# A chunkwise matrix memory: all increments of the state at once in three banks, seven states kept, one denominator step for eight chunks

## The chip, the cores and the metric

The kernel runs on one core of one Trainium2 chip. The metric is the device time of one execution in microseconds (us); lower is better. TensorE (PE) multiplies matrices and transposes, VectorE (DVE) and ScalarE (ACT) work elementwise, GpSimd (POOL) does a little, SyncE (SP) issues the transfers.

## The reference, cut to what matters

Two transformer blocks follow each other on 1024 tokens of width 1024, in float32. The first block has windowed attention beside a matrix memory (mLSTM), then cross attention and a gated feed-forward layer; the second has an RWKV-7 mixer beside banded attention. The change touches the matrix memory alone, which has 4 heads of width 128:

```python
    def step(carry, inp):
        C, n, m = carry
        ...
        num = (w_inter[..., None] * jnp.einsum('bhtd,bhde->bhte', qc, C)
               + jnp.einsum('bhts,bhse->bhte', sc, vc))
        den = w_inter * jnp.einsum('bhtd,bhd->bht', qc, n) + jnp.sum(sc, axis=-1)
        h = num / jnp.maximum(jnp.abs(den), jnp.exp(-m_t))[..., None]
        ...
        C_new = decay[..., None, None] * C + jnp.einsum('bhs,bhsd,bhse->bhde', ws, kc, vc)
```

The output is multiplied by a sigmoid gate, computed as (tanh + 1) / 2, and goes with the attention output into the output projection.

## The kernel before, in words

**The whole.** Projections run as three matmuls each on split operands (float32r, high and low parts), 2400 tiles of lines 1332 to 1334. A planner in Python, `Order`, writes one list of steps; each engine's program goes through that list in order, issues its own part of every step and waits on semaphores. `Order.flow` takes a main stream and side streams. It keeps a clock for each engine (`busy`), moves it by the costs in `work()`, and always asks the stream with the earliest due time for its next steps. A side stream is due again 0.2 us after its last step has ended by those costs. Before a step that needs PSUM, a stream asks `room` and waits until, by the same clocks, so many places are free. The order on each engine thus comes from the cost table, but the waits on the chip are semaphores.

**PSUM.** There are 8 banks of 512 fp32 columns. In the first block banks 0 to 3 are two pairs (`pairs`, for results of 1024 columns), banks 4 to 7 are single (`banks`). Places are handed out first in, first out. A place is given back together with the events that its next user must wait for.

**The matrix memory.** The kernel uses chunks of 128 tokens, 8 of them, and keeps the normalizer `n` as a 129th column of the state: the values in `mva` have a column of ones. The memory starts after all windows of the attention and the gates are done, and the projections of the first stage are done by then, so nothing else runs beside it. Two streams work on heads 0 and 2, and on heads 1 and 3. For every head they emit:

- `ml_e`, `ml_x`: gate rows spread over the partitions by TensorE (line 1490), the exponent's argument by VectorE (2156), exponential by ScalarE (2700)
- `ml_q`: the inter-chunk weights (1499), queries scaled into `PTv` (2164), the eight decay factors (2166)
- `ml_s`: scores of the eight chunks (1511), weighted into `XA` (2172)
- `ml_k`: the keys transposed (1318) and evicted with their weights into `Pv` by ScalarE, in eight instructions (2709)
- the chunk loop: eight times `ml_c` and `ml_h`, below
- `ml_o`: the output turned by eight transposes (1318), gated by VectorE (2207)

In `ml_c` of chunk c TensorE computes the intra-chunk product into one bank (1530), adds query times state to it (1534), and puts the increment, keys times values, into another bank (1540). VectorE copies the first increment (2182) and then makes each new state, decay times old plus increment (2187), in one of four places of `Cb`. ScalarE takes the absolute value of column 128, the denominator (2715). In `ml_h` VectorE takes the maximum with exp(-m) (2195) and the reciprocal (2197), and evicts 128 columns times that times 0.5 (2200).

**Around it.** When all heads are done, SyncE loads x and the memory tokens again (`x_again`), ScalarE and VectorE split the mixed rows (2721, 2213) and the output projection starts.

Of the kernel before, what the change touches and what calls it, by code (L numbers as in the profile page):

```python
# [42 lines left out]
class Signals:  # L43
# [21 lines left out]
    def at(self, name, *event):  # L65
        assert not self.strict or (name, *event) in self.value, (name, event)
        return self.sem(name), self.value.get((name, *event), 1)
# [58 lines left out]
def v3(ap, k):  # L126
    return ap.rearrange("p (k n) -> p k n", k=k)
# [32 lines left out]
class Memory:  # L160
# [38 lines left out]
    def work(self, a, n):  # L199
        return self.f32(W0 + a, n)  # L200
# [16 lines left out]
    def bank(self, b):  # L217
        return self.PS[:, 512 * b:512 * b + 512]
# [21 lines left out]
    def first(self):  # L240
# [22 lines left out]
        self.XA = [self.akT, work(13312, 1024)]  # L263
        self.Cb = [v3(work(31784, 516), 4), v3(work(6144, 516), 4)]
        self.hbuf = [work(0, 1024), work(1024, 1024)]
# [246 lines left out]
def work(step):  # L512
# [31 lines left out]
    if name[:3] == "ml_":  # L544
        return {"ml_e": [("pe", 1.7), ("v", 2.8)], "ml_x": [("a", 1.5)], "ml_q": [("pe", 1.7), ("v", 1.4)],
                "ml_s": [("pe", 1.75), ("v", 1.22)], "ml_k": [("pe", 0.9), ("a", 3.1)], "ml_o": [("pe", 0.9), ("v", 1.22)],
                "ml_c": [("pe", 0.66), ("v", 0.35), ("a", 0.18)], "ml_h": [("v", 0.66)]}[name]
    if name[:6] == "gates_":
# [26 lines left out]
class Order:  # L575
# [260 lines left out]
    def mlstm(self, *heads):  # L836
        for h in heads:
            yield from self.after("att", "gates")
            for first, second, e, f in (("ml_e", "ml_q", ("ml.v", "e", h), ("ml.v", "dec", h)),
                                        ("ml_s", "ml_k", ("ml.v", "sc", h), ("ml.a", "kt", h))):  # L840
                for name, event in ((first, e), (second, f)):
# [4 lines left out]
                    if name == "ml_e":  # L846
                        yield [("ml_x", h)]
            for c in range(8):
                yield from self.room((self.banks, 1 + (c < 7)))
                b, free = self.banks.take()  # L850
                b2, free2 = self.banks.take() if c < 7 else (None, None)
                if c < 7:
                    self.banks.give(b2, ("ml.v", "C", h, c))
                yield [("ml_c", h, c, b, free, b2, free2)]
                self.banks.give(b, ("ml.v", "h", h, c))
                yield [("ml_h", h, c, b)]
            yield from self.room((self.pairs, 1))
# [454 lines left out]
def tensor_program(pe, w, m, S, o):  # L1312
# [208 lines left out]

    def ml_c(h, c, b, free, b2, free2):
        u, sl = h % 2, slice(c * 128, (c + 1) * 128)
        va, num = m.mva[:, c, h, :], bank(b)[:, 0:129]
        w.wait_ge(*at("ml.v", "sc", h))
        w.wait_ge(*at("gemm.a", "ev", "mv1", 3))
        w.wait_ge(*at("ones.g", 0))
        for e in S.each(free):
            w.wait_ge(*e)
        i = pe.matmul(num, m.XA[u][:, sl], va, start=True, stop=(c == 0))  # L1530
        if c:
            w.wait_ge(*at("ml.v", "q", h))
            w.wait_ge(*at("ml.v", "C", h, c - 1))
            i = pe.matmul(num, m.PTv[u][:, sl], m.Cb[u][:, (c + 3) % 4, :], start=False, stop=True)
        i.then_inc(*on("ml.pe", "n", h, c))
        if c < 7:
            w.wait_ge(*at("ml.a", "kt", h))
            for e in S.each(free2):
                w.wait_ge(*e)
            i = pe.matmul(bank(b2)[:, 0:129], m.Pv[u][:, sl], va, start=True, stop=True)  # L1540
            i.then_inc(*on("ml.pe", "kv", h, c))

    def ml_o(h, b, free):
        for e in S.each(free):
            w.wait_ge(*e)
        for c in range(8):
            sl = slice(c * 128, (c + 1) * 128)
            w.wait_ge(*at("ml.v", "h", h, c))
            i = transpose(pair(b)[:, sl], m.hbuf[h % 2][:, sl])
        i.then_inc(*on("ml.pe", "o", h))  # L1550
# [259 lines left out]
    def seq_out(cp, b, free):  # L1810
# [3 lines left out]
        for j in range(4):  # L1814
# [5 lines left out]
              win_t=win_t, win_o=win_o, gates_f=gates_f, gates_t=gates_t, ml_e=ml_e, ml_q=ml_q, ml_s=ml_s, ml_k=ml_k,  # L1820
              ml_c=ml_c, ml_o=ml_o, cross_s=cross_s, cross_t=cross_t, cross_o=cross_o, hs_sum=hs_sum, hs_t=hs_t,
              hs_o=hs_o, band_s=band_s, band_t=band_t, band_o=band_o, lora=lora, prep_m=prep_m, pre_x=pre_x,
# [8 lines left out]
def vector_program(v, w, m, S, o):  # L1831
# [309 lines left out]
    def gates_t(b, free):  # L2141
        w.wait_ge(*at("gates.pe", "t"))
        v.tensor_copy(m.mcs, bank(b)[:, 0:96]).then_inc(*on("gates.v", "mc"))

# [28 lines left out]

    def ml_c(h, c, b, free, b2, free2):
        C = m.Cb[h % 2]
        if c < 7:
            kv = bank(b2)[:, 0:129]
            w.wait_ge(*at("ml.pe", "kv", h, c))
            if c == 0:
                w.wait_ge(*at("alib", 0))  # L2180
                mlstm_free(h)
                v.tensor_copy(C[:, 0, :], kv).then_inc(*on("ml.v", "C", h, c))
            else:
                w.wait_ge(*at("ml.v", "C", h, c - 1))
                w.wait_ge(*at("ml.v", "dec", h))
                w.wait_ge(*at("ml.pe", "n", h, c))
                v.scalar_tensor_tensor(out=C[:, c % 4, :], in0=C[:, (c + 3) % 4, :],
                                       scalar=m.dec[:, 8 * h + c:8 * h + c + 1], in1=kv, op0=MUL, op1=ADD).then_inc(
                    *on("ml.v", "C", h, c))

    def ml_h(h, c, b):
        num = bank(b)[:, 0:129]
        dn = small[:, 416 + 8 * h + c:417 + 8 * h + c]
        w.wait_ge(*at("ml.a", "abs", h, c))
        v.tensor_tensor(dn, dn, m.mc[:, 2, c, h:h + 1], MAX).then_inc(*on("ml.v", "den", h, c))
        w.wait_ge(*at("ml.v", "den", h, c))
        v.reciprocal(dn, dn).then_inc(*on("ml.v", "rcp", h, c))
        w.wait_ge(*at("ml.v", "rcp", h, c))
        mlstm_free(h)
        v.tensor_scalar(m.hbuf[h % 2][:, c * 128:(c + 1) * 128], num[:, 0:128], dn, 0.5, MUL, MUL).then_inc(  # L2200
            *on("ml.v", "h", h, c))

# [294 lines left out]
    def fin_part(h, k, mark):  # L2497
# [8 lines left out]
              gates_log=gates_log, gates_scan=gates_scan, gates_max=gates_max, gates_exp=gates_exp, gates_t=gates_t,  # L2506
              ml_e=ml_e, ml_q=ml_q, ml_s=ml_s, ml_c=ml_c, ml_h=ml_h, ml_o=ml_o, win_p=win_p, mix_part=mix_part, cross_s=cross_s, cross_p=cross_p,
              cross_t=cross_t, cross_o=cross_o, hs_fin=hs_fin, hs_t=hs_t, hs_o=hs_o, band_s=band_s,
# [8 lines left out]
def scalar_program(a, w, m, S, o):  # L2517
# [193 lines left out]

    def ml_c(h, c, b, free, b2, free2):
        dn = small[:, 416 + 8 * h + c:417 + 8 * h + c]
        w.wait_ge(*at("ml.pe", "n", h, c))
        a.activation(dn, bank(b)[:, 128:129], ACT.Abs).then_inc(*on("ml.a", "abs", h, c))

# [126 lines left out]
    def fin_part(h, k, mark):  # L2843
        for e in ("pe", "v", "a"):
            for x in S.upto(e, mark):
# [5 lines left out]
              rms_sum=rms_sum, rms_out=rms_out, last_sum=last_sum, last_out=last_out, ada_c=ada_c, av_t=av_t, win_x=win_x, win_t=win_t, win_o=win_o, gates_f=gates_f,  # L2851
              gates_log=gates_log, gates_exp=gates_exp, ml_x=ml_x, ml_k=ml_k, ml_c=ml_c, mix_part=mix_part,
              cross_x=cross_x, cross_t=cross_t, cross_o=cross_o, hs_sq=hs_sq, hs_fin=hs_fin, band_x=band_x,
# [322 lines left out]
```

## Time and profile before

| | |
|---|---|
| median of 3 runs | 2583.92 us (2582.66 to 2584.40) |
| profiled execution | 2582.81 us, its span 2581.0 us |
| TensorE busy in the span | 2444.9 us, 95% |
| VectorE busy | 1402.0 us, 54% |
| ScalarE busy | 934.5 us, 36% |
| matrix memory | from 375.2 to 461.75 us of the span |

The busy shares are means over stages with different limits. TensorE's busy time counts a matmul as long as it is in the array, at whichever clock was granted, so a busy TensorE may run at half speed. The granted clock is given as a share: 1.00 is 2.4 GHz, 0.50 is 1.2 GHz. A matmul in float32 shows as two records, a transpose as one. Times in the rows are from the start of the span.

### The profile page before, as it was taken

Reading aid. Unit: us, or ns where it says so; the run is one execution under the profiler, and the core shown is the slowest. Engines: PE = TensorE matmul, PEld = TensorE weight load, DVE = VectorE, ACT = ScalarE, POOL = GpSimd, SP = SyncE. Lnnn points to the kernel's source line nnn. Section 1 sums busy time; section 2 is a strip of 40 time slices with the busy share of each in tenths; the row PEclk is TensorE's granted clock in tenths of the full one; section 3 lists DMA queues with packets and bytes.
Section 4 is the critical chain, followed back from the end, with each engine's and each line's share of the span. In section 5 each row is a group of like instructions: output and inputs, shape, how many; then the busy total and the mean of one; then the engine's idle time right before and its main releaser. Section 6 shows DMA issues by size and latency. Waiting matters only on the chain.

```text
span 2581.0 us, 41438 instructions
## 1 busy us (share of the span) xinstructions
PE 2444.9 (95%) x17958; PEld 1968.9 (76%) x17958; DVE 1402.0 (54%) x2515; ACT 934.5 (36%) x1567; POOL 80.1 (3%) x61
## 2 busy tenths in 40 slices
PE   6999988999999999999999999899999998799879
PEld 5777756788888888888888888677777776677657
DVE  4584855665345555543555555563344556667543
ACT  3445432444333333322333423453233232344341
POOL 0000000000000000000000000020000002100100
PEclk9999977999999999999999999899899998899889
DMA  6453310434113333333333343333222212111043
GB/s 193 123 147 108 83 32 1 156 113 133 57 50 88 95 95 98 96 92 98 98 98 98 92 125 93 114 96 106 79 67 67 79 43 68 53 41 41 10 139 115
DMA packets 358191, 230.96 MB, mean 89 GB/s; under 512 B 9461, under 2 KB 332149, under 8 KB 357881
## 3 DMA queue, kind: packets, MB, share of 16 engines
q1 hardware_dynamic: 355272, 222.74, 28.9%
q10 hardware_dynamic: 2736, 5.57, 0.6%
q8 instruction: 142, 2.33, 0.4%
q14 instruction: 41, 0.33, 0.0%
HBM read 210.45 MB, written 17.83 MB: 88 GB/s over the span
## 4 chain that ended last, share of the span: by engine, by line
PE 87%; DVE 7%; ACT 3%; DMA 2%; issue 1%; SPq 0%; ACTq 0%; DVEq 0%
PE PS L1332 21%; PE PS L1333 20%; PE PS L1334 20%; PE PS L1714 5%; PE PS L1318 3%; PE PS L1352 1%; PE PS L1354 1%; PE PS L1353 1%; PE PS L1631 1%; PE PS L1652 1%; PE PS L1585 1%; PE PS L1616 1%; PE PS L1560 1%; PE PS L1597 1%; PE PS L1700 1%
## 5 line engine op out<-in xcount | busy, mean ns | idle before, releaser
L1332 PE MATMUL PS<-SR 128*128 128x512 f32 (+1 forms) x2400 | 956.4, 398 | 39.6 <-DVE SR L1845 35.5
L1333 PE MATMUL PS<-SR 128*128 128x512 f32 (+1 forms) x2400 | 933.7, 389 | 0.0
L1334 PE MATMUL PS<-SR 128*128 128x512 f32 (+1 forms) x2400 | 933.4, 389 | 0.0
L1845 DVE TENSOR_TENSOR SR<-SB,SR 128x1024 fp32r<-128x1024 f32 (+1 forms) x328 | 396.8, 1211 | 387.0 <-ACT SR L2535 386.6
L1332 PEld LDWEIGHTS PS<-SR 128*128 128x128 f32 x2400 | 452.5, 189 | 159.6 <-DVE SR L1845 37.1
L1334 PEld LDWEIGHTS PS<-SR 128*128 128x128 f32 x2400 | 452.4, 188 | 96.2
L1333 PEld LDWEIGHTS PS<-SR 128*128 128x128 f32 x2400 | 453.2, 189 | 89.4 <-issue 1.9
L2535 ACT ACTIVATE SR<-SB 128x1024 fp32r<-128x1024 f32 (+1 forms) x328 | 338.7, 1035 | 276.6 <-DMA SB<-in_w_down 102.8
L1714 PEld LDWEIGHTS PS<-SB 64*64 64x64 f32 x4096 | 127.0, 135 | 36.0 <-issue 21.1
L1714 PE MATMUL PS<-SB 64*64 64x64 f32 x4096 | 139.6, 220 | 9.3 <-DVE SB L2415 5.9
L1318 PE MATMUL PS<-SB 128*128 128x128 f32 (+2 forms) x688 | 106.7, 290 | 27.8 <-DVE SB L2293 11.0
L1318 PEld LDWEIGHTS PS<-SB 128*128 128x128 f32 (+2 forms) x688 | 79.3, 147 | 48.1 <-DVE SB L2293 12.5
L1906 DVE SCALAR_TENSOR_TENSOR SB<-SB 128x512 f32<-128x512 f32 x136 | 102.2, 752 | 4.8
L2542 ACT ACTIVATE SB<-PS 128x512 f32<-128x512 f32 (+1 forms) x71 | 39.0, 572 | 158.2 <-PE PS L1334 120.5
L1881 DVE TENSOR_TENSOR SB<-PS,SB 128x512 f32<-128x512 f32 x48 | 33.1, 690 | 77.2 <-PE PS L1334 77.0
L2581 ACT ACTIVATE SB<-PS 128x512 f32<-128x512 f32 x44 | 26.4, 600 | 132.2 <-PE PS L1334 132.2
L2871 POOL TENSOR_TENSOR SB<-SB 128x512 f32<-128x512 f32 x8 | 16.7, 2086 | 1816.1 <-DVE SB L2325 1816.1
L2776 ACT ACTIVATE SB<-PS 128x640 f32<-128x640 f32 (+4 forms) x64 | 36.0, 569 | 97.6 <-PE PS L1318 97.2
L2593 ACT ACTIVATE SB<-PS 128x512 f32<-128x512 f32 x34 | 20.4, 599 | 120.7 <-PE PS L1334 120.6
L1352 PE MATMUL PS<-SR 128*128 128x512 f32 x160 | 63.0, 394 | 1.0 <-ACT SB L2593 1.0
L1903 DVE TENSOR_SCALAR SB<-SB 128x512 f32<-128x512 f32 x60 | 32.7, 544 | 54.9 <-ACT SB L2581 51.0
L1353 PE MATMUL PS<-SR 128*128 128x512 f32 x160 | 62.3, 390 | 0.0
(261 smaller groups left out, 2509.5 us busy)
## 6 DMA issues: line engine op xcount, KB each, us to landing
SB<-in_w_in SPq DMA_DIRECT2D x110, 512.0 KB, 4.0
SB<-in_w_up SPq DMA_DIRECT2D x88, 512.0 KB, 3.8
SB<-in_w_out SPq DMA_DIRECT2D x32, 512.0 KB, 4.5
SB<-in_w_down SPq DMA_DIRECT2D x32, 512.0 KB, 4.2
SB<-in_w_ada SPq DMA_DIRECT2D x12, 1024.0 KB, 6.4
asides<-SB SPq DMA_DIRECT2D x36, 256.0 KB, 3.3
SB<-in_wkv SPq DMA_DIRECT2D x16, 512.0 KB, 3.9
SB<-in_wq SPq DMA_DIRECT2D x16, 512.0 KB, 4.2
```

The lines of the kernel that those rows point to most:

```text
L1318: return pe.transpose(out, in_, m.I[0:n, 0:n])
L1332: pe.matmul(out, whi[:, k - k0, :], hi[k], start=(k == 0), stop=False)
L1333: pe.matmul(out, whi[:, k - k0, :], lo[k], start=False, stop=False)
L1334: i = pe.matmul(out, wlo[:, k - k0, :], hi[k], start=False, stop=(k == j.K - 1))
L1352: pe.matmul(out, hi, whi[:, k - k0, :], start=(k == 0), stop=False)
L1353: pe.matmul(out, hi, wlo[:, k - k0, :], start=False, stop=False)
L1714: x = pe.matmul(bank(got[a][0])[ps, c:c + 64], lhs(a, q, j)[ps, :], rhs(a, q, j)[ps, :], start=True, stop=True)
L1845: v.tensor_tensor(m.f32r(a, kn * cn), m.f32(a, kn * cn), m.f32r(a + 1024, kn * cn).bitcast(F32), SUB).then_inc(*on("split.v", p))
L1906: v.scalar_tensor_tensor(out=out, in0=pad[:, i:i + 512], scalar=weight(i), in1=out, op0=MUL, op1=ADD).then_inc(*on("conv.v", "tap", j.name ...
L2535: a.activation(m.f32r(at_ + 1024, kn * cn), m.f32(at_, kn * cn), ACT.Copy).then_inc(*on("split.a", p))
L2542: a.activation(j.dst(t), src, j.func, scale=j.scale).then_inc(*on("gemm.a", "ev", j.name, t))
L2776: a.activation(m.PTv3[q][:, 0:W], pair(b)[:, 0:W], ACT.Copy).then_inc(*on("band.a", "pt", j, n, a_))
```

## The change

`ml_c` and `ml_h` are replaced by two steps for each head. `ml_v` computes all seven increments into three banks, three chunks of 129 columns to a bank, and VectorE makes all seven states from them; `Cb` now has seven places for a head. `ml_n` computes the eight numerators, again three to a bank in three banks; ScalarE takes the absolute values of a bank's denominators in one instruction, VectorE does one maximum and one reciprocal on eight columns and evicts a bank in one instruction, with the reciprocals broadcast along the row. The factor 0.5 is gone from that eviction: ScalarE's absolute value has a scale of 2, and the exp(-m) columns are doubled once when the gate columns are copied. The planner's costs are changed accordingly, and the first state copy waits for other events than before, since the longer `Cb` lies over the gate rows. The tables that name the steps for each engine are changed as well and left out here.

```diff
-        self.Cb = [v3(work(31784, 516), 4), v3(work(6144, 516), 4)]
+        self.Cb = [v3(work(31784, 903), 7), v3(work(6144, 903), 7)]
...
-                "ml_c": [("pe", 0.66), ("v", 0.35), ("a", 0.18)], "ml_h": [("v", 0.66)]}[name]
+                "ml_v": [("pe", 1.7), ("v", 2.7)], "ml_n": [("pe", 3.7), ("a", 0.7), ("v", 2.2)]}[name]
...
-            for c in range(8):
-                yield from self.room((self.banks, 1 + (c < 7)))
-                b, free = self.banks.take()
-                b2, free2 = self.banks.take() if c < 7 else (None, None)
-                if c < 7:
-                    self.banks.give(b2, ("ml.v", "C", h, c))
-                yield [("ml_c", h, c, b, free, b2, free2)]
-                self.banks.give(b, ("ml.v", "h", h, c))
-                yield [("ml_h", h, c, b)]
+            for name, event in (("ml_v", "bank"), ("ml_n", "h")):
+                yield from self.room((self.banks, 3))
+                got = [self.banks.take() for _ in range(3)]
+                for i in range(3):
+                    self.banks.give(got[i][0], ("ml.v", event, h, i))
+                yield [(name, h, got)]
...
-    def ml_c(h, c, b, free, b2, free2):
-        u, sl = h % 2, slice(c * 128, (c + 1) * 128)
-        va, num = m.mva[:, c, h, :], bank(b)[:, 0:129]
-        w.wait_ge(*at("ml.v", "sc", h))
+    def ml_v(h, got):
+
+        u = h % 2
+        w.wait_ge(*at("ml.a", "kt", h))
         w.wait_ge(*at("gemm.a", "ev", "mv1", 3))
         w.wait_ge(*at("ones.g", 0))
-        for e in S.each(free):
-            w.wait_ge(*e)
-        i = pe.matmul(num, m.XA[u][:, sl], va, start=True, stop=(c == 0))
-        if c:
-            w.wait_ge(*at("ml.v", "q", h))
-            w.wait_ge(*at("ml.v", "C", h, c - 1))
-            i = pe.matmul(num, m.PTv[u][:, sl], m.Cb[u][:, (c + 3) % 4, :], start=False, stop=True)
-        i.then_inc(*on("ml.pe", "n", h, c))
-        if c < 7:
-            w.wait_ge(*at("ml.a", "kt", h))
-            for e in S.each(free2):
-                w.wait_ge(*e)
-            i = pe.matmul(bank(b2)[:, 0:129], m.Pv[u][:, sl], va, start=True, stop=True)
-            i.then_inc(*on("ml.pe", "kv", h, c))
+        for c in range(7):
+            b, free = got[c // 3]
+            if c % 3 == 0:
+                for e in S.each(free):
+                    w.wait_ge(*e)
+            i = pe.matmul(bank(b)[:, 129 * (c % 3):129 * (c % 3) + 129], m.Pv[u][:, 128 * c:128 * c + 128], m.mva[:, c, h, :],
+                          start=True, stop=True)
+            if c in (2, 5, 6):
+                i.then_inc(*on("ml.pe", "kv", h, c // 3))
+
+    def ml_n(h, got):
+        u = h % 2
+        w.wait_ge(*at("ml.v", "sc", h))
+        w.wait_ge(*at("ml.v", "q", h))
+        for c in range(8):
+            b, free = got[c // 3]
+            num, sl = bank(b)[:, 129 * (c % 3):129 * (c % 3) + 129], slice(c * 128, (c + 1) * 128)
+            if c % 3 == 0:
+                for e in S.each(free):
+                    w.wait_ge(*e)
+            i = pe.matmul(num, m.XA[u][:, sl], m.mva[:, c, h, :], start=True, stop=(c == 0))
+            if c:
+                w.wait_ge(*at("ml.v", "C", h, c - 1))
+                i = pe.matmul(num, m.PTv[u][:, sl], m.Cb[u][:, c - 1, :], start=False, stop=True)
+            if c in (2, 5, 7):
+                i.then_inc(*on("ml.pe", "n", h, c // 3))
 
     def ml_o(h, b, free):
         for e in S.each(free):
             w.wait_ge(*e)
         for c in range(8):
             sl = slice(c * 128, (c + 1) * 128)
-            w.wait_ge(*at("ml.v", "h", h, c))
+            w.wait_ge(*at("ml.v", "h", h, c // 3))
             i = transpose(pair(b)[:, sl], m.hbuf[h % 2][:, sl])
         i.then_inc(*on("ml.pe", "o", h))
 
...
     def gates_t(b, free):
         w.wait_ge(*at("gates.pe", "t"))
-        v.tensor_copy(m.mcs, bank(b)[:, 0:96]).then_inc(*on("gates.v", "mc"))
+        v.tensor_copy(m.mcs[:, 0:64], bank(b)[:, 0:64]).then_inc(*on("gates.v", "mc0"))
+        v.tensor_scalar(m.mcs[:, 64:96], bank(b)[:, 64:96], 2.0, None, MUL).then_inc(*on("gates.v", "mc"))
...
-    def ml_c(h, c, b, free, b2, free2):
+    def ml_v(h, got):
         C = m.Cb[h % 2]
-        if c < 7:
-            kv = bank(b2)[:, 0:129]
-            w.wait_ge(*at("ml.pe", "kv", h, c))
+        for c in range(7):
+            kv = bank(got[c // 3][0])[:, 129 * (c % 3):129 * (c % 3) + 129]
+            w.wait_ge(*at("ml.pe", "kv", h, c // 3))
             if c == 0:
-                w.wait_ge(*at("alib", 0))
+                for e in S.upto("pe", "g"):
+                    w.wait_ge(*e)
+                w.wait_ge(*at("gates.a", "i", 1))
+                w.wait_ge(*at("gates.pe", "f"))
                 mlstm_free(h)
-                v.tensor_copy(C[:, 0, :], kv).then_inc(*on("ml.v", "C", h, c))
+                i = v.tensor_copy(C[:, 0, :], kv).then_inc(*on("ml.v", "C", h, c))
             else:
                 w.wait_ge(*at("ml.v", "C", h, c - 1))
                 w.wait_ge(*at("ml.v", "dec", h))
-                w.wait_ge(*at("ml.pe", "n", h, c))
-                v.scalar_tensor_tensor(out=C[:, c % 4, :], in0=C[:, (c + 3) % 4, :],
-                                       scalar=m.dec[:, 8 * h + c:8 * h + c + 1], in1=kv, op0=MUL, op1=ADD).then_inc(
-                    *on("ml.v", "C", h, c))
-
-    def ml_h(h, c, b):
-        num = bank(b)[:, 0:129]
-        dn = small[:, 416 + 8 * h + c:417 + 8 * h + c]
-        w.wait_ge(*at("ml.a", "abs", h, c))
-        v.tensor_tensor(dn, dn, m.mc[:, 2, c, h:h + 1], MAX).then_inc(*on("ml.v", "den", h, c))
-        w.wait_ge(*at("ml.v", "den", h, c))
-        v.reciprocal(dn, dn).then_inc(*on("ml.v", "rcp", h, c))
-        w.wait_ge(*at("ml.v", "rcp", h, c))
+                v.scalar_tensor_tensor(out=C[:, c, :], in0=C[:, c - 1, :], scalar=m.dec[:, 8 * h + c:8 * h + c + 1], in1=kv,
+                                       op0=MUL, op1=ADD).then_inc(*on("ml.v", "C", h, c))
+            if c in (2, 5, 6):
+                S.also("ml.v", "bank", h, c // 3)
+
+    def ml_n(h, got):
+
+        dn = small[:, 416 + 8 * h:424 + 8 * h]
+        w.wait_ge(*at("ml.a", "abs", h, 2))
+        v.tensor_tensor(dn, dn, m.mc[:, 2, :, h], MAX).then_inc(*on("ml.v", "den", h))
+        w.wait_ge(*at("ml.v", "den", h))
+        v.reciprocal(dn, dn).then_inc(*on("ml.v", "rcp", h))
+        w.wait_ge(*at("ml.v", "rcp", h))
         mlstm_free(h)
-        v.tensor_scalar(m.hbuf[h % 2][:, c * 128:(c + 1) * 128], num[:, 0:128], dn, 0.5, MUL, MUL).then_inc(
-            *on("ml.v", "h", h, c))
+        for i in range(3):
+            n = 3 if i < 2 else 2
+            num = v3(bank(got[i][0])[:, 0:129 * n], n)[:, :, 0:128]
+            v.tensor_tensor(v3(m.hbuf[h % 2][:, 384 * i:384 * i + 128 * n], n), num,
+                            dn[:, 3 * i:3 * i + n].unsqueeze(2).to_broadcast([128, n, 128]), MUL).then_inc(*on("ml.v", "h", h, i))
...
-    def ml_c(h, c, b, free, b2, free2):
-        dn = small[:, 416 + 8 * h + c:417 + 8 * h + c]
-        w.wait_ge(*at("ml.pe", "n", h, c))
-        a.activation(dn, bank(b)[:, 128:129], ACT.Abs).then_inc(*on("ml.a", "abs", h, c))
+    def ml_n(h, got):
+        for i in range(3):
+            n = 3 if i < 2 else 2
+            w.wait_ge(*at("ml.pe", "n", h, i))
+            a.activation(small[:, 416 + 8 * h + 3 * i:416 + 8 * h + 3 * i + n], v3(bank(got[i][0])[:, 0:129 * n], n)[:, :, 128], ACT.Abs,
+                         scale=2.0).then_inc(*on("ml.a", "abs", h, i))
```

## Rows read from the trace of the kernel before

**Rows 1.** The page, the chain that ended last: share of the span by engine.
```profile
PE 87%; DVE 7%; ACT 3%; DMA 2%; issue 1%; SPq 0%; ACTq 0%; DVEq 0%
```

**Rows 2.** Busy time by stretch: us, busy us of PE, PEld, DVE, ACT, POOL, clock, DMA share, GB/s.
```profile
375.00:397.50 22.50, 22.06 (x68) 12.82 (x65) 9.36 (x22) 3.77 (x9) 0.00 (x0) 0.58 0.00 1
397.50:419.00 21.50, 17.92 (x107) 14.64 (x104) 14.66 (x64) 5.49 (x28) 0.00 (x0) 0.92 0.00 0
419.00:438.80 19.80, 19.30 (x64) 11.60 (x65) 10.49 (x24) 3.38 (x8) 0.00 (x0) 0.66 0.00 1
438.80:461.80 23.00, 18.15 (x107) 14.71 (x104) 15.80 (x64) 5.50 (x28) 0.00 (x0) 0.93 0.00 1
```

**Rows 3.** The chain in order of time (start us, us, what), one period of the chunk loop.
```profile
405.99 0.35 DVE SB L2187
406.33 0.08 DVE SB L2195
406.44 0.17 DVE SB L2197
406.64 0.36 DVE SB L2200
407.00 0.04 issue
407.04 0.49 PE PS L1530 x2
407.53 0.22 PE PS L1534 x2
407.76 0.44 PE PS L1540 x2
```

**Rows 4.** Groups of instructions from 375 to 461.8 us, columns as in the page's part 5.
```profile
L2200 DVE TENSOR_SCALAR SB<-PS,SB 128x128 f32<-128x128 f32 x32 | 11.2, 351 | 1.1
L2187 DVE SCALAR_TENSOR_TENSOR SB<-SB,PS 128x129 f32<-128x129 f32 x24 | 8.3, 345 | 4.9 <-PE PS L1540 4.9
...
L2715 ACT ACTIVATE SB<-PS 128x1 f32<-128x1 f32 x32 | 5.5, 186 | 26.8 <-PE PS L1534 26.8
```

**Rows 5.** The timeline: start us, us, engine, line, operation, count.
```profile
375.20 7.19 PE L1490 MATMUL PS<-SB 4*128 4x512 f32 x8
...
398.46 0.49 PE L1540 MATMUL PS<-SB 128*128 128x129 f32 x2 [0.51 <-ACT SB L2709]
400.53 0.49 PE L1540 MATMUL PS<-SB 128*128 128x129 f32 x2 [1.36 <-ACT SB L2715]
401.24 0.64 PE L1534 MATMUL PS<-SB 128*128 128x129 f32 x2
401.67 0.64 PE L1540 MATMUL PS<-SB 128*128 128x129 f32 x2
...
419.06 4.94 PE L1490 MATMUL PS<-SB 4*128 4x512 f32 x8 [0.57 <-DVE SB L2207]
...
439.76 0.49 PE L1540 MATMUL PS<-SB 128*128 128x129 f32 x2 [0.50 <-ACT SB L2709]
...
459.41 2.34 DVE L2207 SCALAR_TENSOR_TENSOR SB<-SB,PS 128x1024 f32<-128x1024 f32 x2
```

**Rows 6.** Groups of VectorE over the whole span, tensor_tensor from PSUM at two widths.
```profile
L2393 DVE TENSOR_TENSOR SB<-PS,SB 128x512 f32<-128x512 f32 x16 | 10.3, 685 | 7.0 <-PE PS L1700 6.9
L2430 DVE TENSOR_TENSOR SB<-PS,SB 128x256 f32<-128x256 f32 x80 | 30.1, 418 | 38.1 <-PE PS L1714 38.1
```

**Rows 7.** Busy time by stretch of 1 us, columns as in rows 2.
```profile
399.00:400.00 1.00, 0.17 (x2) 0.00 (x0) 0.28 (x1) 1.00 (x6) 0.00 (x0) 1.00 0.00 0
401.00:402.00 1.00, 1.00 (x7) 1.00 (x5) 0.88 (x5) 0.09 (x1) 0.00 (x0) 0.50 0.00 0
405.00:406.00 1.00, 1.00 (x8) 0.87 (x8) 0.64 (x4) 0.17 (x1) 0.00 (x0) 1.00 0.00 0
421.00:422.00 1.00, 1.00 (x3) 0.33 (x2) 0.92 (x4) 0.00 (x0) 0.00 (x0) 0.69 0.00 0
```

More of the change, by code:

```diff
@@ L1820, in tensor_program @@
               win_t=win_t, win_o=win_o, gates_f=gates_f, gates_t=gates_t, ml_e=ml_e, ml_q=ml_q, ml_s=ml_s, ml_k=ml_k,
-              ml_c=ml_c, ml_o=ml_o, cross_s=cross_s, cross_t=cross_t, cross_o=cross_o, hs_sum=hs_sum, hs_t=hs_t,
+              ml_v=ml_v, ml_n=ml_n, ml_o=ml_o, cross_s=cross_s, cross_t=cross_t, cross_o=cross_o, hs_sum=hs_sum, hs_t=hs_t,
               hs_o=hs_o, band_s=band_s, band_t=band_t, band_o=band_o, lora=lora, prep_m=prep_m, pre_x=pre_x,
@@ L2506, in vector_program @@
               gates_log=gates_log, gates_scan=gates_scan, gates_max=gates_max, gates_exp=gates_exp, gates_t=gates_t,
-              ml_e=ml_e, ml_q=ml_q, ml_s=ml_s, ml_c=ml_c, ml_h=ml_h, ml_o=ml_o, win_p=win_p, mix_part=mix_part, cross_s=cross_s, cross_p=cross_p,
+              ml_e=ml_e, ml_q=ml_q, ml_s=ml_s, ml_v=ml_v, ml_n=ml_n, ml_o=ml_o, win_p=win_p, mix_part=mix_part, cross_s=cross_s, cross_p=cross_p,
               cross_t=cross_t, cross_o=cross_o, hs_fin=hs_fin, hs_t=hs_t, hs_o=hs_o, band_s=band_s,
@@ L2851, in scalar_program @@
               rms_sum=rms_sum, rms_out=rms_out, last_sum=last_sum, last_out=last_out, ada_c=ada_c, av_t=av_t, win_x=win_x, win_t=win_t, win_o=win_o, gates_f=gates_f,
-              gates_log=gates_log, gates_exp=gates_exp, ml_x=ml_x, ml_k=ml_k, ml_c=ml_c, mix_part=mix_part,
+              gates_log=gates_log, gates_exp=gates_exp, ml_x=ml_x, ml_k=ml_k, ml_n=ml_n, mix_part=mix_part,
               cross_x=cross_x, cross_t=cross_t, cross_o=cross_o, hs_sq=hs_sq, hs_fin=hs_fin, band_x=band_x,
```

## The prediction

> **What bounds the kernel now.** I read the page first: the chain that ended last is 87% TensorE and 7% VectorE [rows 1], so in most of the span a saving on VectorE is worth nothing. It is worth something only where the chain leaves TensorE. The changed steps are the matrix memory of the first block, which runs from 375 to 461.8 us with no projection beside it; I therefore took the busy times by stretch there [rows 2]. The memory goes twice through a front (rows of gates, scores, evictions; TensorE busy 22.1 of 22.5 and 19.3 of 19.8 us) and a chunk loop (21.5 and 23.0 us). In the chunk loops TensorE is "busy" 17.9 and 18.2 us, VectorE 14.7 and 15.8, and no DMA moves. The chain in order of time settles which counts [rows 3]: a period serves one chunk of both heads and is 408.22 - 405.99 = 2.23 us long; half of it is state update, maximum, reciprocal, eviction on VectorE, the other half three matmuls that wait for that eviction's bank. VectorE's own work in a period is 2 x (0.345 + 0.351 + 0.31) = 2.0 us (the two means from [rows 4], the two small ones from the 0.31 us between 406.33 and 406.64 in [rows 3]). The loop is bound by VectorE and by the ping-pong over banks. TensorE's share is much smaller: a dense fp32 matmul (two records) starts every 0.22 to 0.25 us at the full clock [rows 3], 0.43 at the lower level [rows 5].
>
> **The change, part by part.** I write times after the moment at which the scaled keys of the first head of a pair are ready: 398.46 us, the first key-value matmul [rows 5]. From there to the start of the next front (419.06, released by the gated output of head 0) it is 20.60 us now. In the second pair it is 439.76 to 459.41 + 2.34 - 1.14 = 460.61, 20.85 us; 1.14 us for the other head's gated output follows in both kernels (2.34 for two, each 1.2 long with a small overlap).
>
> Prices: a matmul 0.23 full, 0.43 low; from the start of a last matmul to its reader 0.49 + 0.04 = 0.53 [rows 3, 5]; a state update that waits for the one before it 0.345 + 0.04 = 0.385 [rows 3, 4]; an Abs 0.19 [rows 4], with its wait 0.23; a maximum and a reciprocal in a row 0.4 (0.31 on the chain, without the overlap of 0.08). The new eviction (tensor_tensor from three chunks of a bank, the denominator broadcast) has no row: at 256 elements tensor_tensor from PSUM takes 0.418 us and at 512 0.685 [rows 6], so 384 elements lie between, 0.55 on the line; broadcasting is taken at nothing, and if it cost twice as much (the far end: 0.685 for 384) it would be 0.4 us a head. Three of them are 0.55 + 0.55 + 0.42 less a small overlap, 1.4 us. Removed against that are 8 x (0.351 + 0.31) = 5.3 us per head.
>
> Increments: seven matmuls of head 0 run without a wait (three banks of four are free). The first bank can be read at 2 x 0.23 + 0.53 = 1.0; seven states take 0.33 + 6 x 0.385 = 2.65 and end at 3.65. Head 1 starts at 400.53, that is 2.07, when its keys are evicted [rows 5]; two of its banks are released by head 0's states in time, and its states follow on VectorE: 3.65 + 2.65 = 6.3. Those 14 copies and updates are not new work; they were in the loop.
>
> Outputs: from the planner's costs I worked out the order on TensorE: increments 0, increments 1, outputs 0, outputs 1, turn 0, turn 1, then the next front. Outputs 0 have 15 matmuls and no state to wait for: its first bank is free at 3.65, so 3.7 + 15 x 0.23 = 7.15 (its last bank, freed by head 1's sixth state at 5.9, is in time). Result 0.3 later, Abs 0.23, denominators 0.4: 8.1; evictions to 9.5. Outputs 1: five matmuls to 8.3, then the wait for a bank until head 0's first eviction, 8.1 + 0.55 + 0.04 = 8.7, then ten to 11.0; + 0.3 + 0.23 + 0.4 = 11.95, evictions to 13.35, gated output of head 0 1.14: 14.5. The transposes of head 0 lie under outputs 1's denominators, and what is queued behind outputs 1's waits on TensorE are only those transposes, which nobody needs before 13.35. ScalarE loses 26 of 32 reads and was waiting all along.
>
> Thus at the full clock a pair saves 20.6 - 14.5 = 6.1 and 20.85 - 14.5 = 6.35 us, together 12.45. The clock takes some back. After TensorE's sparse stretch at 399 to 400 us it is at 0.50 from 401 to about 404 and back at 1.00 at 405 [rows 7]. If the same dip remains, 2.7 us at half speed, some seven matmuls cost 0.2 more each of which bank waits absorb part: 0.8 us a pair. The changed order fills that sparse stretch with increments, so I take half, 0.4 a pair. The second front now begins at full clock and loses it 2 to 3 us on (0.69 at 421 to 422 [rows 7]); its first group takes 4.94 us against 7.19 in the first front [rows 5]. TensorE now idles before it longer (11.9 to 14.5 but for eight transposes), so up to 2.2 us are at stake; I take a third, 0.7. Sum: 12.45 - 0.8 - 0.7 = 10.9 us.
>
> The rest at nothing: the gate columns are copied in two instructions instead of one while VectorE waits for the first front; the doubling moved into a copy and Abs's scale costs no instruction on the path; the new waits of the first state copy (end of projection, gate rows) are for events before 375 us, and on VectorE only the states are queued behind them. Seven kept states need 903 columns, no transfer. DMA: the x and memory loads and the mixed rows' splits are released by the end of the memory, so they move with it; the output projection behind it starts at the same distance. Its banks come in another order; I price that at 0, from -1 to +1 us.
>
> Profiled execution: 2582.81 us for a span of 2581.0; the median of the runs is 2583.92, 1.11 above it. 2582.81 - 10.9 = 2571.9; on the median 2573.0. I forecast 2573.
>
> The Trainium skill speaks against such a scheme: TensorE: Matmul & The Clock Gate, "A second HAM failure mode: psum-queue depth-cycling", says that a kernel which cycles through PSUM banks idles shortly between groups of matmuls so often that the clock swings between its levels. The trace before has such short waits too, in every period, and 1.00 at 405 to 406 us with TensorE busy throughout [rows 7]. By that rule the first rival below would hold, 2589; by the row the forecast.
>
> **The rivals.** (1) *The lower clock governs* (slower). The outputs wait for banks and reads in groups; if TensorE falls to 1.2 GHz for the whole stretch, it bounds it: 44 matmuls x 0.43 = 18.9, + 0.3 + 0.23 + 0.4 + 1.4 + 1.14 = 22.4 us a pair, 1.8 and 1.55 over now, and the second front's first group 2.2 more: 2583.92 + 5.5 = 2589.5. For it: the dip at 401 to 404 and both fronts at 0.50 to 0.66 on average [rows 2, 7]. Against it: 0.92 and 0.93 in the loops, whose matmuls were thinner in time than the new ones. It decides from a duration: 44.8 us at the low level cost 12.45 + 3.35 = 15.8, 0.35 us each; with 2.2 gone at the front nothing is left of 12.45 from 10.25 / 0.35 = 29 us on.
> (2) *The gain is half size*: bank waits in series (each head's outputs take three of four banks) add a full eviction group, 1.4 us, and its read and denominators, 0.9, to each pair, and the front loses its 2.2 us: 12.45 - 4.6 - 2.2 = 5.6, 2578.3. For it: one pair of heads now shares four banks in groups of three. Against: the walk above, where only one wait of 0.4 us is left.
> (3) *The gain is given back behind it*: the output projection waits for w_out, x or the mixed rows, or the planner's next stage comes out in a worse order: 2583.9, no change. For it: no row here shows that stage. Against it: by the code those loads and splits start from the end of the memory itself, and no DMA moves in the loops that could be late [rows 2].
> (4) *The changed order doesn't arise* (a head's outputs behind the next one's front): about +1 us a pair against the forecast, 2575, inside the range.
>
> **How the numbers follow.** Forecast with (4): 0.82. Half size: 0.09. Given back: 0.05. Lower clock: 0.04. A change of under 0.2%, 5.2 us, can't be told from none here, so faster means below 2578.7: 0.82 + 0.08 of the half-size case = 0.90; same 0.01 + 0.05 = 0.06; slower 0.04. The unknown costs: dips from 0 to 2 x 0.8, front from 0 to 2.2, eviction up to 2 x 0.8 more, order of banks +-1. Best: 12.45 + 1 and 0.6 of spread in the runs, 2569.8. Worst of these: 12.45 - 1.6 - 2.2 - 1.6 - 1 = 6.05, 2577.9. Range 2569.5 to 2578.
>
> **What would show it.** Right: after 398.5 seven key-value matmuls in 1.6 us; the pair ends (next front's start) near 413, the memory near 450; VectorE's busy time in a chunk loop falls from 14.7 by about 7 us; evictions of 384 elements near 0.55 us; clock near 1.00 while outputs run. Wrong: a clock of 0.50 over the outputs, or TensorE waiting on evictions for more than a us per pair; a front of the next pair ahead of outputs; or a span that falls less than the end of the memory moves.

## The result, and the profile after

| | before | after |
|---|---|---|
| median of 8 runs | 2584.47 us (2582.66 to 2594.98) | 2568.40 us (2564.30 to 2578.75) |
| profiled execution, its span | 2582.81, 2581.0 us | 2568.16, 2566.4 us |
| memory, first gate row to last gated output | 86.55 us | 73.93 us |
| the rest of the span | 2494.4 us | 2492.5 us |

The ratio is 0.9938, 95% interval 0.9918 to 0.9958: faster by 16 us in the median. I had forecast 2573 within 2569.5 to 2578, so the time lies 1.1 us under the range. Inside the memory the forecast was nearly exact at the full clock; what it took off for the clock was not lost, and some 3 us came from outside the memory.

The busy times by stretch, after (columns as in [rows 2]: us, busy us of PE, PEld, DVE, ACT, POOL, clock, DMA share, GB/s):

```profile
376.60:399.90 23.30, 22.18 (x66) 12.90 (x64) 9.37 (x22) 4.67 (x12) 0.00 (x0) 0.59 0.00 1
399.90:414.30 14.40, 12.87 (x104) 11.78 (x104) 9.28 (x26) 3.09 (x14) 0.00 (x0) 1.00 0.00 1
414.30:435.00 20.70, 19.54 (x64) 11.38 (x64) 10.48 (x23) 4.28 (x11) 0.00 (x0) 0.67 0.00 1
435.00:450.50 15.50, 12.88 (x104) 11.78 (x104) 10.37 (x26) 3.10 (x14) 0.00 (x0) 0.99 0.01 1
```

The fronts (first and third row) are as long as before: 23.3 and 20.7 us. The two loops lost 6.2 and 6.5 us. VectorE is busy 9.3 us in the first loop, where it was 14.7 [rows 2]; that is 5.4 us less, where I had named about 7, because my 0.31 us for the two small steps and 0.351 us for an eviction held short gaps and overlaps that the busy time doesn't count. The granted clock is 1.00 where it was 0.92. The memory starts 1.4 us later than before because of a low clock level ahead of it, in code that is the same in both (at 351 to 358 us the granted clock is 0.76 before and 0.56 after).

The chain in order of time through the first pair's loop, after; it answers to [rows 3]:

```profile
402.01 1.83 PE PS L1530 x14
403.84 0.59 PE PS L1545 x4
404.42 0.22 PE PS L1548 x2
...
407.10 0.24 PE PS L1548 x2
407.34 0.02 issue
407.36 0.18 ACT SB L2732
407.54 0.02 issue
407.56 0.18 DVE SB L2208
407.75 0.02 issue
407.77 0.21 DVE SB L2210
407.99 0.02 issue
408.01 0.57 DVE SB L2216
408.58 0.04 issue
408.62 0.49 PE PS L1545 x2
...
411.57 0.21 DVE SB L2210
411.78 0.02 issue
411.81 1.35 DVE SB L2216 x3
413.16 1.14 DVE SB L2223
414.30 0.04 issue
414.34 0.69 PE PS L1487
```

L1530 is the increments of head 1, L1545 and L1548 are the outputs, L2732 Abs, L2208 the maximum, L2210 the reciprocal, L2216 the evictions, L2223 the gated output, L1487 the next front. Where VectorE stood in the chain once in every period of the loop [rows 3], it stands there twice a pair: from 407.56 to 408.58, because outputs 1 (of the pair's second head) wait for the bank that head 0's first eviction frees, and from 411.36 on, behind all outputs. The offsets of the walk are read from the timeline's rows; these are the increments of the first head and VectorE's copies and states of both heads:

```profile
399.94 1.83 PE L1530 MATMUL PS<-SB 128*128 128x129 f32 x14 [0.72 <-ACT SB L2725]
400.92 0.29 DVE L2195 COPY SB<-PS 128x129 f32<-128x129 f32 x1 [2.85 <-PE PS L1530]
401.25 2.41 DVE L2199 SCALAR_TENSOR_TENSOR SB<-SB,PS 128x129 f32<-128x129 f32 x6
...
403.57 0.29 DVE L2195 COPY SB<-PS 128x129 f32<-128x129 f32 x1
...
403.89 2.41 DVE L2199 SCALAR_TENSOR_TENSOR SB<-SB,PS 128x129 f32<-128x129 f32 x6
```

And the groups of VectorE from 399 to 450.6 us, after, for the new eviction, which had no row before (columns as in [rows 4]):

```profile
L2216 DVE TENSOR_TENSOR SB<-PS,SB 128x384 f32<-128x384 f32 x8 | 4.1, 553 | 0.1
L2216 DVE TENSOR_TENSOR SB<-PS,SB 128x256 f32<-128x256 f32 x4 | 1.7, 416 | 0.0
```

0.553 us for 384 elements against 0.55 forecast: the broadcast costs nothing.

### The profile page after: what moved, and what is told of

The parts are those of the page before. It is cut to its first block, busy times and chain, and to the rows that moved or that the text cites. A ratio compares the mean times of both kernels' runs of the same rounds, so it can differ in the third digit from the quotient of the medians.

```text
span 2566.4 us, 41351 instructions
## 1 busy us (share of the span) xinstructions
PE 2430.7 (95%) x17958; PEld 1959.8 (76%) x17958; DVE 1391.3 (54%) x2440; ACT 931.0 (36%) x1547; POOL 80.0 (3%) x61
## 4 chain that ended last, share of the span: by engine, by line
PE 87%; DVE 7%; ACT 3%; DMA 2%; issue 1%; SPq 0%; ACTq 0%; DVEq 0%
PE PS L1329 21%; PE PS L1330 20%; PE PS L1331 20%; PE PS L1723 5%; PE PS L1315 3%; PE PS L1349 1%; PE PS L1640 1%; PE PS L1351 1%; PE PS L1350 1%; PE PS L1661 1%; PE PS L1594 1%; PE PS L1569 1%; PE PS L1625 1%; PE PS L1606 1%; DVE SR L1854 1%
## 5 line engine op out<-in xcount | busy, mean ns | idle before, releaser
L2599 ACT ACTIVATE SB<-SB 128x512 f32<-128x512 f32 x44 | 27.8, 632 | 95.3 <-DVE SB L1915 95.3
```

## The experiments

Each kernel was timed beside the kernel before. Means here are over all runs of a kernel, with their standard error (+-); the kernel before was timed 89 times in all (mean 2585.6 +- 0.3), the changed kernel 25 times (2570.0 +- 0.8). "Memory" is read from the timeline of each trace as above.

| kernel | memory, us | runs | mean, us | mean less memory |
|---|---|---|---|---|
| before | 86.55, 86.50 | 89 | 2585.6 +- 0.3 | 2499.1 |
| changed | 73.93, 73.95, 73.92, 73.82 | 25 | 2570.0 +- 0.8 | 2496.1 |
| changed, padded by 10 squarings | 86.54 | 11 | 2585.4 +- 1.3 | 2498.9 |
| changed, padded by 5 | 80.36 | 12 | 2580.4 +- 1.1 | 2500.0 |
| changed, padded by 2 | 76.52 | 9 | 2576.6 +- 1.4 | 2500.1 |
| denominators for each bank | 71.43, 71.29 | 11 | 2572.1 +- 0.6 | 2500.7 |
| denominators and evictions for each chunk | 83.55 | 12 | 2581.8 +- 0.3 | 2498.2 |
| increments at once only | 85.99 | 12 | 2585.9 +- 1.4 | 2499.9 |
| gap ahead of head 1's states | 84.23 | 12 | 2583.1 +- 1.4 | 2498.9 |

**The kernel before, again.**

> The kernel before once more, for its spread and for a second trace. The profiled execution of before had the memory from 375.2 to 461.75 us, 86.55 us, with the low clock level in two short dips inside the chunk loops. Theory A (the change is worth what the memory gets shorter, 12.6 us; the other 3.4 us of the measured 16 are where TensorE's low clock level happens to fall in the rest of the program, which differs from execution to execution): runs spread by several us with a median of 2583 to 2587, longer runs have a lower mean granted clock, and the memory in the second trace takes 85 to 89 us. Theory B (before is systematically slower outside the memory too): its time outside the memory is again some 2.5 to 3.5 us longer than after's.

Median 2584.65 of 11 runs, ratio to its own kind 1.0009 (1.0000 to 1.0019). Memory 86.50 us, but the rest of this span 2500.2, 5.8 us longer than in the first trace of the same kernel, with a mean granted clock of 0.963 against 0.968. So 16 us between two medians of eight runs can't be read as 16 us of one stage.

**The changed kernel, again, three times.**

> The changed kernel once more. Theory A: memory 73.9 us within 1 us, median 2568 to 2573 (12.6 below before, within 2), runs spread over 10 us or more in step with the mean granted clock. Theory B: the median stays at 2568 or below, 16 us under before, also with more runs, and the time outside the memory is again shorter than before's by 2.5 to 3.5 us.

Median 2568.84 of 5, ratio 0.9944 (0.9931 to 0.9956). Memory 73.95.

> The changed kernel a third time: memory 73.9 us within 0.2; the time outside the memory, so far 2492.5 and 2495.7 us for it and 2494.4 and 2500.2 for the kernel before, anywhere from 2489 to 2505. If a systematic gain hides outside the memory (theory B), it is below 2494 again and the median is 2568 or less; by theory A the median is 2568 to 2573.

Median 2569.31 of 6, ratio 0.9940 (0.9922 to 0.9959), rest 2495.7. The first eight runs show what moves them: 2564.30 and 2564.76 us had a granted clock of 0.971, 2568.1 to 2568.6 had 0.969 to 0.970, 2577.91 and 2578.75 had 0.963.

> The changed kernel once more beside these three, on the same chip. Theory A: its mean of these runs alone comes back to 2572.7 within 2; theory B: stays at 2569.8 or below. Memory 73.9 us.

Median 2570.68 of 6, mean 2570.5 +- 1.7, ratio 0.9943 (0.9926 to 0.9959): between what the two theories said, nearer B (theory A said 2572.7 within 2). Memory 73.82.

**The gain put back as idle time.**

> The changed kernel with ten squarings of 128x1024 on VectorE in a row ahead of the last two gated outputs; about 1.25 us each, so the memory ends 12.5 us later, as late as before, and nothing else is changed (they compute nothing that is used). Theory A: time as before, ratio 1.000 within 0.0015, 2583 to 2586 us. Theory B (a gain that doesn't come from the memory's length): stays 3 us or more faster than before, 2578 to 2581.

```diff
+        if h == 3:
+            for i in range(10):
+                w.wait_ge(*at("ml.v", "h", h, 2) if not i else at("ml.v", "pad", i - 1))
+                v.tensor_tensor(m.XA[1], m.hbuf[1], m.hbuf[1], MUL).then_inc(*on("ml.v", "pad", i))
```

The timeline of VectorE, padded kernel:

```profile
445.49 1.35 DVE L2216 TENSOR_TENSOR SB<-PS,SB 128x384 f32<-128x384 f32 x3
446.88 12.56 DVE L2221 TENSOR_TENSOR SB<-SB 128x1024 f32<-128x1024 f32 x10
459.35 2.34 DVE L2227 SCALAR_TENSOR_TENSOR SB<-SB,PS 128x1024 f32<-128x1024 f32 x2
```

Memory 86.54 us, median 2584.10, ratio 1.0007 (0.9996 to 1.0018). With the memory as long as before, the time is that of before, although every instruction of the change is in place. The whole gain goes with the memory's length, and none of it is left when that is given back. The 12.6 us of padding cost 15.4 +- 1.5 us in the means, as the change had gained 15.6 +- 0.9, so the 3 us outside the memory went too.

> The changed kernel with two of the ten squarings of the padded run, so the memory ends 2.5 us later (76.4 us). Open so far: the changed kernel (mean of 19 runs 2569.8) is 15.5 +- 1.1 us under before (mean of 69 runs 2585.3), while its memory is 12.6 shorter; the kernels with other lengths of the memory lie at before's time minus the difference in length, within 1.5 us. Theory A (chance of where the low clock level falls): mean 2585.3 - 10.1 = 2575.2, within 2. Theory B (the changed kernel itself has some 3 us more outside the memory, which the padded run lost for another reason): 2569.8 + 2.5 = 2572.3.

> Five squarings, 6.25 us, memory 80.2 us. Theory A: mean 2585.3 - 6.35 = 2579.0 within 2. Theory B: 2569.8 + 6.25 = 2576.0.

The same edit with 2 and 5 squarings. Ratios 0.9963 (0.9948 to 0.9979) and 0.9979 (0.9969 to 0.9990); means 2576.6 +- 1.4 and 2580.4 +- 1.1. Theory A said 2575.2 and 2579.0, theory B 2572.3 and 2576.0: both lie nearer A. B is off by 4.3 and 4.4 us, which is 2.4 and 3 standard errors when the error of its starting point (2569.8, 19 runs, some 1.1) is counted too. Beside the six runs of the changed kernel from the same round alone (mean 2570.5 +- 1.7), B would say 2573.1 and 2576.9 and is off by 3.5 us with an error of 2. So these runs speak against a fixed 3 us in the changed code, but don't settle it.

**What denominators and evictions for several chunks at once are worth.**

> The changed kernel with the shared denominators undone: increments at once and numerators three to a bank stay, but VectorE again takes maximum, reciprocal and eviction for each chunk (8 x 0.65 us a head in place of 1.75). By the walk VectorE then bounds a pair: states to 6.35 us after the first scaled keys, two times 5.2 for the outputs, 1.14 for the gated output, 17.9 to 18.0 in place of 14.4: memory 73.9 + 7.1 = 81 us, time 7 above the changed kernel. Rival (the outputs were paced by TensorE's bank waits, not by VectorE): memory within 2 us of 73.9. This tells what the shared denominators are worth: near 7 of the 12.6 us by the first, near nothing by the second.

```diff
-        v.tensor_tensor(dn, dn, m.mc[:, 2, :, h], MAX).then_inc(*on("ml.v", "den", h))
...
+        for c in range(8):
+            i = c // 3
+            dn = small[:, 416 + 8 * h + c:417 + 8 * h + c]
+            w.wait_ge(*at("ml.a", "abs", h, i))
+            v.tensor_tensor(dn, dn, m.mc[:, 2, c, h:h + 1], MAX).then_inc(*on("ml.v", "den", h, c))
...
+            e = v.tensor_scalar(m.hbuf[h % 2][:, c * 128:(c + 1) * 128], num, dn, 1.0, MUL, MUL)
```

Median 2582.05, ratio 0.9986 (0.9977 to 0.9995). Busy times by stretch of this kernel (first front, first loop, second front, second loop):

```profile
376.90:400.30 23.40, 22.23 (x66) 12.93 (x65) 9.36 (x22) 4.72 (x12) 0.00 (x0) 0.59 0.00 1
400.30:418.20 17.90, 13.56 (x104) 11.94 (x104) 15.12 (x64) 3.05 (x14) 0.00 (x0) 0.95 0.00 0
418.20:441.50 23.30, 22.09 (x65) 12.81 (x65) 10.48 (x23) 4.39 (x12) 0.00 (x0) 0.60 0.00 1
441.50:460.50 19.00, 13.51 (x104) 11.88 (x104) 16.25 (x64) 2.99 (x14) 0.00 (x0) 0.92 0.00 1
```

The loop of the first pair is 17.9 us, as the walk said, and VectorE busy 15.1 of them. The edit gives each chunk back not only its maximum and reciprocal but its own eviction too (8 x 0.35 us a head for 1.35), so it prices both together: 3.5 us a pair, 7 of the 12.6. How the 7 divide between the two no run shows. What this kernel keeps of the change, above all the increments at once, still takes 2.7 us out of the first loop and 3.0 out of the second, against the kernel before. The memory is 83.55, not 81, and the mean time 11.8 us above the changed kernel, not 7: the second front is 23.3 us where the changed kernel has 20.7. From 413 to 417 us TensorE is busy 0.13 to 0.42 us in each us, the granted clock is 0.76 in the last of them and 0.50 behind it, and the second front's first group takes 7.19 us (4.94 before [rows 5], 5.45 in the changed kernel):

```profile
418.24 7.19 PE L1487 MATMUL PS<-SB 4*128 4x512 f32 x8 [0.44 <-DVE SB L2223]
```

This is the term of "up to 2.2 us" that I had priced at 0.7: here it is paid whole, in the changed kernel not as time (its front is 20.7 us, as before).

**What the increments at once are worth alone.**

> Increments at once and seven states kept, but the outputs as before the change: one bank and one Abs, maximum, reciprocal and eviction for each chunk. VectorE has the same work as in the run with a denominator for each chunk, so by my walk the memory is again 81 us, within 1: grouping numerators in banks is worth nothing by itself. Rival (grouping counts: a bank per chunk brings back a TensorE-VectorE round trip for each): memory 83 us or more, up to the 86.5 of before.

```diff
+            for c in range(8):
+                yield from self.room((self.banks, 1))
+                b, free = self.banks.take()
+                yield [("ml_n", h, c, b, free)]
+                self.banks.give(b, ("ml.v", "h", h, c))
+                yield [("ml_h", h, c, b)]
```

Median 2585.55, ratio 1.0000 (0.9986 to 1.0013), memory 85.99 us. That is the rival's number, but not for its reason: no round trip is back, VectorE evicts one chunk every 0.65 us from 407.4 to 417.3. The planner ordered the end of the pair otherwise, as VectorE's timeline shows:

```profile
417.69 1.22 DVE L2221 SCALAR_TENSOR_TENSOR SB<-SB,PS 128x1024 f32<-128x1024 f32 x1 [0.42 <-PE PS L1320]
418.83 0.15 DVE L2209 TENSOR_TENSOR SB<-SB 128x1 f32<-128x1 f32 x1
419.01 0.17 DVE L2211 RECIPROCAL SB<-SB 128x1 f32<-128x1 f32 x1
419.22 0.35 DVE L2214 TENSOR_SCALAR SB<-PS,SB 128x128 f32<-128x128 f32 x1
...
419.60 2.16 DVE L2167 SCALAR_TENSOR_TENSOR SB<-PS,SB 128x128 f32<-128x128 f32 x8
421.68 1.21 DVE L2221 SCALAR_TENSOR_TENSOR SB<-SB,PS 128x1024 f32<-128x1024 f32 x1
```

Head 1's last chunk (L2209 to L2214) comes behind head 0's gated output (L2221), and its own gated output behind the next front's first work (L2167), 4 us after head 0's. So this run doesn't price the grouping of numerators cleanly: increments at once with outputs chunk by chunk bring 0.6 us of memory and nothing in the time in this order, and how much is order and how much clock was not taken apart.

**A gap in TensorE's work.**

> The changed kernel with three squarings of 128x1024 (3.75 us) on VectorE ahead of the states of the second head of each pair, which nothing uses; TensorE stands still behind them. If the granted clock stays at 1.00 in the loop, as it did in both traces of the changed kernel, the memory gets 2 x 3.7 longer, 81.4 us. If an idle stretch of this size brings the low level (the first term that I took off the sum), the outputs behind it run at 0.50 for a while and a pair gets up to 2 us more: 82.5 to 85 us.

```diff
+        if h % 2:
+            mlstm_free(h)
+            for i in range(3):
+                w.wait_ge(*at("ml.v", "q", h) if not i else at("ml.v", "gap", h, i - 1))
+                v.tensor_tensor(m.hbuf[1], m.mqk[h], m.mqk[h], MUL).then_inc(*on("ml.v", "gap", h, i))
+            w.wait_ge(*at("ml.v", "gap", h, 2))
```

Memory 84.23 us, 10.3 above the changed kernel for 7.5 of inserted work: beyond it the two loops lose 1.3 and 1.1 us and the second front 0.4. Median 2584.04, ratio 0.9990 (0.9976 to 1.0004). The stretches of 2 us around the gap:

```profile
404.00:406.00 2.00, 0.43 (x4) 0.24 (x3) 1.93 (x3) 0.17 (x1) 0.00 (x0) 1.00 0.00 0
406.00:408.00 2.00, 0.20 (x1) 0.20 (x2) 1.79 (x5) 0.00 (x0) 0.00 (x0) 1.00 0.00 0
408.00:410.00 2.00, 2.00 (x13) 2.00 (x13) 1.25 (x4) 0.00 (x0) 0.00 (x0) 0.66 0.00 0
410.00:412.00 2.00, 2.00 (x11) 2.00 (x11) 0.05 (x1) 0.35 (x2) 0.00 (x0) 0.50 0.00 0
412.00:414.00 2.00, 2.00 (x17) 1.85 (x17) 1.68 (x5) 0.17 (x1) 0.00 (x0) 0.99 0.00 0
```

TensorE stands nearly still from 404 to 408 us; the level falls only when it is busy again, and the outputs behind it take the 1.3 us longer. So the first term I took off (0.8 a pair, half of it in the sum) was a real mechanism. It came here behind some 4 us of near idleness, and the changed kernel has no wait in its loops above 0.7 us. The Trainium skill says the same in TensorE: Matmul & The Clock Gate, "HAM oscillation — how this bites in real kernels": work after an idle wait starts at the low level. The trace agrees but for the first part of a us, since 408 to 410 us has 0.66 and not 0.50. What the Trainium skill warns of on the same page, "A second HAM failure mode: psum-queue depth-cycling", the first rival's rule, is not borne out by the changed kernel: its loops have waits of 0.2 to 0.7 us, and the granted clock is 1.00 and 0.99.

**Denominators for each bank.**

> The changed kernel with the maximum and the reciprocal taken for each bank as soon as its Abs is there, three pairs of small instructions a head in place of one. By my walk through the loop outputs 1 no longer waits for a bank (its first eviction ends 1 us earlier) and behind the last Abs only one bank is left to evict (0.4 + 0.42 in place of 0.4 + 1.35): a pair ends 1.45 us earlier, 2.9 in all, memory 71 us, time 2.9 under the changed kernel. Rival: the two more small pairs (0.4 us each) on VectorE eat it, memory 73.5 to 75 us, no difference.

```diff
+        for i in range(3):
+            n = 3 if i < 2 else 2
+            part = dn[:, 3 * i:3 * i + n]
+            w.wait_ge(*at("ml.a", "abs", h, i))
+            v.tensor_tensor(part, part, m.mc[:, 2, 3 * i:3 * i + n, h], MAX).then_inc(*on("ml.v", "den", h, i))
...
```

Memory 71.43 us, 2.5 shorter (forecast 2.9), but the time did not follow: median 2572.63 of 5, ratio 0.9952 (0.9939 to 0.9964).

> Maximum and reciprocal for each bank, once more. Its memory was 71.43 us, 2.5 shorter than the changed kernel's, but its five runs had a mean of 2571.6, no faster. Theory A: memory 71.4 again, mean 2585.3 - 15.1 = 2570.2 within 2, and the changed kernel beside it at 2572.7 within 2 once there are enough runs. Theory B: 2.5 us below the changed kernel's 2569.8, 2567.3.

Median 2573.16 of 6, ratio 0.9951 (0.9937 to 0.9964), memory 71.29. The shorter memory is plain in both traces and the time is not shorter: mean 2572.1 +- 0.6 against 2570.0 +- 0.8. The second round alone, 2572.5, is above what either theory said (2570.2 within 2, and 2567.3). Part of it is seen behind the memory. In this kernel the low level comes once more, 108 us after its end; the stretches of this kernel (first fence) and of the changed kernel's fourth trace (second fence):

```profile
500.00:556.00 56.00, 53.75 (x276) 45.64 (x275) 32.08 (x42) 23.80 (x38) 0.00 (x0) 1.00 0.39 112
556.00:560.00 4.00, 4.00 (x24) 4.00 (x22) 3.66 (x6) 2.22 (x4) 0.00 (x0) 0.57 0.08 22
```

```profile
556.00:560.00 4.00, 3.12 (x26) 3.13 (x27) 4.00 (x6) 1.69 (x4) 0.00 (x0) 1.00 0.46 126
```

Its steps are 1.3 us later from there on, counted from the end of the memory. It beats the kernel before, but not the changed kernel.

## Why the prediction was right or wrong

*The bound.* Right. VectorE and the ping-pong paced the loop; giving VectorE back its eight small steps and eight evictions a head costs 7 of the 12.6 us.

*The walk through a pair.* Right to 0.2 us. From the first scaled key: states of head 0 begin at 1.0 (measured 0.98), outputs 1 wait until 8.7 (8.68), head 1's evictions end at 13.35 (13.22), next front at 14.5 (14.40). Second pair: 435.05 to 449.39, 14.34. The order on TensorE and VectorE was the one worked out, and rivals (2) and (4) fell with it. Savings 6.20 and 6.51 against 6.1 and 6.35.

*The step that failed inside the memory: what the clock takes back.* The sum has a term for the clock, 1.5 us in all. I took 0.8 us off for a dip in the two loops and 0.7 for the second front. The loops ran at 1.00 and 0.99, and the second front is 20.7 us in both kernels: the level still falls in it, but its first group is 0.5 us slower (5.45 against 4.94 [rows 5]), its scores 0.5 faster (5.37 against 5.86), because the level was back sooner. The rows are first group and scores after (first fence) and the scores before (second fence):

```profile
414.34 5.45 PE L1487 MATMUL PS<-SB 4*128 4x512 f32 x8 [0.69 <-DVE SB L2223]
...
426.55 5.37 PE L1508 MATMUL PS<-SB 128*128 128x128 f32 x32
```

```profile
430.76 5.86 PE L1511 MATMUL PS<-SB 128*128 128x128 f32 x32
```

The term measured 0, and the memory lost 12.6 us instead of 10.9. I had seen that the dip at 401 us comes behind a stretch where TensorE is nearly idle [rows 7] and that the increments fill it, and kept half of its price all the same.

*The step that failed outside it: what lies behind the memory.* I had priced it at 0, from -1 to +1 us, and allowed 0.6 us for the spread of runs, so the range ended at 2569.5. The runs of the changed kernel spread over 16 us, in step with the mean granted clock, and 2584.47 - 12.6 = 2571.9 is what the memory alone explains. The measured median is 3.5 us below that in the first eight runs; over 25 runs and the 89 of before the means are 15.6 +- 0.9 apart, 3 us more than the memory. In the four rounds in which both kernels were timed side by side the means are 16.1, 14.4, 16.2 and 16.0 us apart, each time more than 12.6. Every other kernel of the table has 2498.2 to 2500.7 us outside its memory, the changed one 2496.1. The forecast was 4.6 us too high: 1.5 of it is the clock's term, 0.3 the walk, 3.5 lie here, and 0.6 goes off because the median before is 2584.47 over eight runs and was 2583.92 over the three I started from. No step of the prediction foresaw the 3.5.

The traces show where executions part, though not why. From the memory's end to the end of the span the four traces of the changed kernel take 2115.9, 2119.4, 2119.1 and 2115.7 us and the two of before 2119.3 and 2123.3. Over the first 1180 us behind the memory the mean granted clock is 1.00 in all six (a few us at the low level in the first 20 hide in that mean). They part mostly in later stages, which are the same in both kernels, and most of all 1950 to 2050 us behind the memory's end; here are the changed kernel's first trace (first row) and the second of the kernel before (second row):

```profile
2400.50:2500.50 100.00, 73.16 (x588) 55.47 (x587) 52.11 (x120) 42.35 (x80) 4.44 (x4) 0.88 0.26 85
2413.40:2513.40 100.00, 75.14 (x540) 55.63 (x537) 48.63 (x114) 39.49 (x78) 4.45 (x4) 0.73 0.22 74
```

In that stretch the changed kernel has 0.88 in three traces and 0.81 in the fourth, the kernel before 0.86 and 0.73. One kernel's own executions thus differ there by as much as the two kernels do. Whether the changed kernel meets the low level less often by something in its timing, or by chance in 25 runs, this part stays open.

*The rivals.* (1) fell: 1.00. (3) fell for the changed kernel. The kernel with denominators for each bank did give 2.5 us back behind its memory, but what its traces show of it, 1.3 us, is a low clock level and not the waits that (3) names.

## What to carry to other kernels

Where two engines hand single chunks to each other through a few banks, put everything that depends on nothing first (here all increments of the state), keep all intermediate states, and do the small per-chunk steps once for all chunks and evict several chunks at once: eight reciprocals of one column cost 8 x 0.16 us, one of eight columns 0.2. Cost a clock dip only where the new order still has the idle stretch ahead of it. Read a stage's gain from that stage's own trace, which repeats to 0.13 us here, and give the whole time the spread that the runs show, here 16 us.

## What the runs showed of the hardware

- The low clock level comes late: in the run with the gap TensorE was nearly idle (0.63 us busy of 4) from 404 to 408 us at a granted 1.00 and busy from 408 to 412 at 0.66 and 0.50. The cost falls on the work behind the idle stretch, 1.3 us in that loop.
- Executions of one kernel differ by up to 16 us on the same instructions (2562.82 at a mean granted clock of 0.972, 2578.75 at 0.963), while the stage of 74 us in it repeats within 0.13 us.
- tensor_tensor from PSUM with a stride of 129 columns between runs of 128, and with one operand broadcast, keeps its rate: 0.553 us for 384 elements, 0.416 for 256, where plain operands take 0.418 [rows 6].
